# Expert weight slabs asked for in two transfers, of 120 and of 8 partitions, in place of one of 128

## The reference, cut to what matters

```python
def swiglu(h, wg, wu, wd):
    return (jax.nn.silu(h @ wg) * (h @ wu)) @ wd

def moe_ffn(h, w_router, wg, wu, wd):
    ...
    def one_block(args):
        xe, e = args
        return swiglu(xe, wg[e], wu[e], wd[e])
    yb = lax.map(one_block, (xb, blk_e)).reshape(m, D_MODEL)
```

## Time and profile before

| | |
|---|---|
| three runs | 1571.83 us median, 1565.4 to 1572.04 |
| profiled execution, its own time | 1569.43 us |
| span from first to last instruction | 1567.7 us |
| granted TensorE clock, mean | 0.986 |
| TensorE matmuls busy | 1461.3 us, 93% of the span |
| moved by DMA | 398.49 MB, mean 254 GB/s |
| chain that ended last | 91% TensorE, 5% issue, 2% DVE, 1% DMA |

### The profile page before, as it was taken

One profiled execution on the slowest core, in us unless ns is written; L12 is line 12 of the kernel. 1 busy time (PEld: TensorE's weight loads), 2 busy tenths in 40 slices (PEclk: granted clock), 3 DMA queues, 4 the chain that ended last, 5 costly groups with the idle time before them and its releaser, 6 DMA issues.

```text
span 1567.7 us, 44059 instructions
## 1 busy us (share of the span) xinstructions
PE 1461.3 (93%) x20574; PEld 1212.6 (77%) x20574; DVE 282.6 (18%) x705; ACT 203.5 (13%) x530; POOL 130.3 (8%) x200
## 2 busy tenths in 40 slices
PE   6999999999999999999999889997899988888987
PEld 5667666666666667767998889997799978888986
DVE  2354720000000245464100000000000000000012
ACT  1245410000000024532000000000000000000000
POOL 3221116000000011111100000000000000000010
PEclk9999999999999999999999999999999999999999
DMA  9933338993323523342899999999999999999991
GB/s 249 254 114 106 110 112 286 364 320 127 123 82 119 137 85 91 95 132 94 285 396 379 360 366 349 346 340 352 349 352 361 383 352 364 334 358 346 355 375 62
DMA packets 197689, 398.49 MB, mean 254 GB/s; under 512 B 11922, under 2 KB 67866, under 8 KB 197344
## 3 DMA queue, kind: packets, MB, share of 16 engines
q1 hardware_dynamic: 180720, 346.38, 64.3%
q0 software_dynamic: 15216, 46.34, 9.3%
q10 hardware_dynamic: 1568, 2.91, 0.7%
HBM read 360.00 MB, written 37.57 MB: 254 GB/s over the span
## 4 chain that ended last, share of the span: by engine, by line
PE 91%; issue 5%; DVE 2%; DMA 1%; ACT 0%; SPq 0%; ACTq 0%; DVEq 0%
PE bank L1328 30%; PE bank L1350 15%; PE bank L1233 13%; PE bank L784 7%; PE bank L1250 6%; PE bank L767 2%; PE bank L1097 2%; PE bank L1080 2%; PE bank L753 1%; PE bank L1052 1%; PE bank L1064 1%; PE bank L738 1%; PE bank L707 1%; DMA arena<-in_x_sample 1%; PE bank L1364 1%
## 5 line engine op out<-in xcount | busy, mean ns | idle before, releaser
L1328 PE MATMUL bank<-arena,ring 128*64 128x108 f32 (+7 forms) x11264 | 478.2, 247 | 51.7 <-issue 51.4
L1328 PEld LDWEIGHTS bank<-arena,ring 128*64 128x64 f32 x11264 | 467.9, 138 | 62.0 <-issue 61.1
L1350 PE MATMUL bank<-arena,ring 128*64 128x108 f32 (+7 forms) x5632 | 242.4, 249 | 27.5 <-issue 27.5
L1350 PEld LDWEIGHTS bank<-arena,ring 128*64 128x64 f32 x5632 | 236.9, 140 | 32.1 <-issue 31.9
L1233 PE MATMUL bank<-hnT,ring 128*128 128x336 f32 x704 | 199.1, 446 | 1.8 <-DVE hnT L1712 1.8
L1233 PEld LDWEIGHTS bank<-hnT,ring 128*128 128x128 f32 x704 | 133.8, 190 | 67.1 <-issue 2.3
L784 PE MATMUL bank<-hnT,ring 128*128 128x336 f32 x384 | 120.1, 458 | 0.0
L2195 DVE TENSOR_TENSOR arena<-arena,bank 128x432 f32<-128x432 f32 (+15 forms) x48 | 24.6, 513 | 469.5 <-PE bank L1328 469.4
L1250 PE MATMUL bank<-arena,ring 128*128 128x336 f32 x352 | 99.6, 446 | 0.0
L784 PEld LDWEIGHTS bank<-hnT,ring 128*128 128x128 f32 x384 | 70.8, 193 | 35.0 <-issue 7.0
L1250 PEld LDWEIGHTS bank<-arena,ring 128*128 128x128 f32 x352 | 67.0, 190 | 32.5
(11 more groups left out here) (387 smaller groups left out, 1071.2 us busy)
## 6 DMA issues: line engine op xcount, KB each, us to landing
ring<-in_moe_w_gate SPq DMA_DIRECT2D x88, 1024.0 KB, 7.6
ring<-in_moe_w_up SPq DMA_DIRECT2D x88, 1024.0 KB, 7.5
ring<-in_moe_w_down SPq DMA_DIRECT2D x88, 1024.0 KB, 6.8
ring<-in_w_in SPq DMA_DIRECT2D x16, 1024.0 KB, 6.8
ring<-in_w_gate SPq DMA_DIRECT2D x11, 1024.0 KB, 10.4
ring<-in_w_up SPq DMA_DIRECT2D x11, 1024.0 KB, 15.8
xg_rows<-arena POOLq DMA_DIRECT2D x1, 11200.0 KB, 48.5
y_rows<-arena POOLq DMA_DIRECT2D x1, 11200.0 KB, 89.4
```

The source lines that it names most:

```text
L1328: ins = mm(into[part, rows * fi:rows * fi + rows], weights[:, c, col:col + 64], xg[:, k0 + c, :], start=(k0 + c == 0 and fi == 0), stop=(k ...
L1350: ins = mm(bank[5 + c // 4][part, rows * (c % 4):rows * (c % 4) + rows], weights[:, col:col + 64], hid[:, f, :], start=(f == 0 and c % 4 = ...
```

## The change

Each slab of the experts is asked for in two transfers. The first writes partitions 0 to 119 of the slot, and the second, right behind it, partitions 120 to 127. Both raise the slot's semaphore by 16, so that a whole slab now counts 32, and TensorE's waits ask for that. The bytes, the pieces of a partition and the order of the slabs stay as they are. The slabs of the mixers and of the dense layer, and the transfers of token rows, are not touched.

```diff
 RING, SLAB = 11, 2048
+PARTS = 2
...
                         src = a["moe_w_down"][0, e, r0:r0 + 256, :].rearrange("(r p) n -> p r n", p=128)
-                    sp.dma_start(dst, src).then_inc(slab_here[s], 16)
+                    for part in (slice(0, 120), slice(120, 128)):
+                        sp.dma_start(dst[part, :, :], src[part, :, :]).then_inc(slab_here[s], 16)
...
-                            pe.wait_ge(slab_here[s], k * (16 * FFN_SLABS // RING) + (fixed_seen[s] + 16 * (j // RING + 1)))
+                            pe.wait_ge(slab_here[s], k * (16 * PARTS * FFN_SLABS // RING) + (fixed_seen[s] + 16 * PARTS * (j // RING + 1)))
...
-                        pe.wait_ge(slab_here[s], k * (16 * FFN_SLABS // RING) + (fixed_seen[s] + 16 * (j // RING + 1)))
+                        pe.wait_ge(slab_here[s], k * (16 * PARTS * FFN_SLABS // RING) + (fixed_seen[s] + 16 * PARTS * (j // RING + 1)))
```

## The result

The changed kernel takes 2081.11 us (median of three, 2076.32 to 2086.82) against 1571.83 us. The measured ratio is 1.329, with a 95% interval of 1.324 to 1.334; the quotient of these two medians is 1.324, at the lower end of the interval. The direction was forecast, the size was not: 1890 us was the number and 2030 us the top of the range.

What follows compares the result with a forecast made beforehand. TensorE and the DMA engines were taken to lie close, slabs over about 3.15 us making transfers the bound. 779.8 us + 246 slabs x 4.33 us = 1845, plus 27, 2.7, 12.8 and 1.7, gave 1889, so 1890 us; range 1550 to 2030.

Steps and rivals of the forecast that it cites:

- What bounds the kernel now: Experts' stage: TensorE and DMA engines lie close; TensorE waits 79 us for instructions, SP has 620 us of slack.
- the limit of about 3 us: Experts' stage: a slab taking longer than about 3.15 us makes the transfers the bound of the whole stage.
- The extra issues cost nothing: SP's queue: 264 added issues at 0.37 us, 98 us in all, lie inside SP's 620 us of waiting.
- What a slab costs: Expert slabs: between 2.67 and 4.88 us each, taken as 1.049/242 = 4.33 us from the 112-partition token rows.
- the dip of the token rows: Around the 112-partition token-row transfer the rate falls from near 400 to 208 to 296 GB/s; 242 GB/s inside it.
- the two rivals: Expert slabs, nine rows on some engines: instructions on a free engine, 1564 us, chance 0.22; on a nine-row engine, 1648 us, 0.06.
- the likeliest case: Expert slabs slow down to between 3.2 and 4.88 us each, 1614 to 2030 us in all, 1890 us predicted; chance 0.66.
- The bound of 4.88 us: Expert slabs: the most a slab costs, 1.049/215, if 120 partitions behave as 64; gives 2030 us in all.
- The sum: Whole kernel: 779.8 + 246 x 4.33 = 1845 us, plus 27, 2.7, 12.8 and 1.7 us, together 1889 us.
- The faster rival: Experts' stage: one engine carries no slab, only instructions, so TensorE's 79 us of rests go; 1564 us, chance 0.22.
- What the profile would show: Experts' stage: 220 to 260 GB/s, engines 9 tenths busy, TensorE 6 or 7, landings over 20 us, hardly any SP waits.
- The engine share near 15/16: Experts' stage: with rests near nothing and about 350 GB/s, a sign that one engine is left to instructions; chance 0.22.

## Why the prediction was wrong in size

- *What bounds the kernel now*: right. SP's slack was there, extra 128-partition transfers cost nothing, and with slabs of 4.4 us and more the stage went by the slabs. No run lies between 2.7 and 4.4 us for all slabs, so the limit of about 3 us itself wasn't tried. The waits named the slabs in the kernel after.
- *The extra issues cost nothing*: right, by the run with two transfers of 128. In the kernel after an issue of a gate slab's part took 1.6 us at the median in place of 0.37, probably because the queue was full. That too was foreseen, and foreseen to cost nothing.
- *What a slab costs*: **this step failed**, the term "4.33 us". Two rows of the timeline of the kernel after carry it, SP's first issues of the stretch and TensorE's last experts' matmuls (start and length in us):

```profile
789.36 3.02 SPq L489 DMA_DIRECT2D ring<-in_moe_w_up  x4
...
2053.42 5.67 PE L1352 MATMUL bank<-arena,ring 128*64 128x96 f32 x128 [0.23 <-DMA ring<-in_moe_w_down]
```

The last ends at 2059.1, and with 14 token and result transfers at 213 GB/s (30 us) and 2.9 us for the last slab this leaves (2059.1 - 2.9 - 30 - 789.4)/246 = 5.03 us. The 120 rows alone took 4.41 us by the same sum, and 112 and 16, with eight rows on each of 16 engines, 4.44 us. So the dip of the token rows had priced the pace of the packets almost rightly, 0.1 us too low. The eight rows are what was missing. I spread the slab's bytes at one rate, as if the extra transfer were part of the first. Eight of the engines carry nine rows, so the factor 9/8 that I gave to the two rivals belonged in the likeliest case as well: 4.41 x 9/8 = 4.96 us. The rest is 0.07 us. It fits packets that are a little slower still: one of q1 (share x 16 engines x length / packets) took 0.930 x 16 x 1245/117175 = 0.158 us here and 0.956 x 16 x 1087/107919 = 0.154 us with 120 partitions alone. The share shows the uneven load, though not in full: if seven of the 15 engines waited for the eight with nine rows, I would expect 95.6 x 128/135 = 90.6%, and it read 93.0%.
- *The bound of 4.88 us*: too low for the same reason. It was the 64-partition rate with even load. With nine rows on an engine it would have been 4.88 x 9/8 = 5.5 us, and the range would have held the result.
- *The sum*: 172 of the 187 us between 1889 and the profiled 2076.3 are this term. SP resumes 9.6 us later, the token and result transfers make 3 us, and the end 3 us.
- *The faster rival*: it needed the 120-partition transfer to be free of the slowdown, and it isn't. Whether the instructions' engine was left alone stays open. With the stage bound by slabs, waits for instructions before line 1330 fell to 16.5 us, and no run frees an engine while slabs stay at full rate.
- *What the profile would show*: the 220 to 260 GB/s came out as about 210, TensorE's 6 to 7 tenths came, the landings over 20 us were seen with 120 partitions alone. SP's waits before line 489 for the matmuls of line 1330 came to 52.6 us, where 431.5 stood before. The engine share near 15/16, which I had named as a sign of the faster rival, came too, without its speed: it shows that an engine is idle, and not what the others are worth. TensorE's clock did fall. It read 0.84 from 1300 to 1500 us, the window's last column but two (the columns are length, then PE, PEld, DVE, ACT and POOL with their instructions, then clock, DMA share and GB/s):

```profile
1300.00:1500.00 200.00, 131.92 (x2384) 125.09 (x2384) 5.31 (x10) 4.71 (x10) 0.52 (x1) 0.84 0.95 206
```

In it, 64 matmuls took up to 4.64 us in the timeline above in place of 2.49. A slab took longer still, so it was mostly covered; what it adds to the time wasn't tried.

## What to carry to other kernels

Where weights stream at the full rate of the DMA engines, ask for them in transfers of 128 partitions (none of the splits tried here, from 120 and 8 down to sixteen of 8, kept the full rate); cut a transfer along the row if it must be cut. One transfer of another height slows the stream around it too, so small side transfers in such a stage are worth padding to 128 (0.35% here for seven of them). When a transfer is split, price both effects and multiply them, the pace of a packet and the rows on the fullest engine. For 120 and 8 this gives 4.96 us per slab against 5.03 measured; for 104 and 24 it gave 2190 us in all against 2151.

## What the runs showed that I had not expected

- A stream of 16-partition transfers runs at 224 GB/s, hardly less than one of 64 and 64 (230), though each of them covers an eighth of SBUF's partitions.
- The pace of an engine differs with how many others are at work and with the height of the transfers: 18.9 GB/s each for eight, about 14 for sixteen, 24.1 for sixteen in transfers of 128.
- TensorE loses 79 us to its own instructions before the change, 5% of the time, behind slabs in the same DMA engines. The trace bears out that these are waits for instructions: from 779 to 1530 us TensorE has 57 rests of over 0.4 us, and each of them ends 1.24 to 1.60 us after a packet of queue q8 has ended. Splitting each slab into two transfers of 128 partitions left it at 53.3 + 26.3 = 80 us, by the waits of that run (total, times, longest):

```profile
PE bank L1331 <- issue: 53.3, 45, 3.6
...
PE bank L1353 <- issue: 26.3, 26, 2.6
```
